# Score steps that divide blocks by four in place of six lower levels, in a chunked gated-linear-attention step on one core

## What is computed

```python
b = jnp.cumsum(gc, axis=2)
decay = jnp.exp(jnp.where(causal, b[:, :, :, None, :] - b[:, :, None, :, :], -jnp.inf))
scores = jnp.einsum('bhtd,bhsd,bhtsd->bhts', qc, kc, decay)
...
c = _split_cols(h @ w_in[l])
...
x = x + _rmsnorm(mix @ w_out[l], norm_post[l])
```

## Time and profile before

| | |
|---|---|
| median of 3 runs | 1036.46 us (1035.76 to 1039.31) |
| the profiled execution, its own time | 1035.77 us |
| its span in the profile | 1033.9 us |
| PE, DVE, ACT, POOL busy, share of the span | 96%, 58%, 42%, 36% |
| one middle tile (425.25 to 542.24 us) | 116.99 us |
| granted clock of PE over the span | 0.985 |

### The profile page before, as it was taken

One profiled execution on the slowest core, in us unless ns is written; L12 is line 12 of the kernel. 1 busy time (PEld: TensorE's weight loads), 2 busy tenths in 40 slices (PEclk: granted clock), 3 DMA queues, 4 the chain that ended last, 5 costly groups with the idle time before them and its releaser, 6 DMA issues.

```text
span 1033.9 us, 26901 instructions
## 1 busy us (share of the span) xinstructions
PE 992.6 (96%) x11652; PEld 737.4 (71%) x11652; DVE 594.5 (58%) x1047; ACT 434.0 (42%) x845; POOL 376.0 (36%) x510
## 2 busy tenths in 40 slices
PE   2997899999999999999999999999999999999997
PEld 2867577855886668865887668865887668866783
DVE  4997578635744466535745467445735467335564
ACT  6965454531533335431534325432534325333333
POOL 1224441174305550174305650174305641256200
PEclk9997699999999999999999999999999999999999
DMA  8820432001220013101220013101220013001011
GB/s 309 292 92 3 135 121 61 9 1 42 63 62 1 2 63 65 39 2 42 63 62 1 2 63 62 42 1 42 63 62 2 2 62 59 25 2 42 1 65 44
DMA packets 41527, 56.21 MB, mean 54 GB/s; under 512 B 27793, under 2 KB 28603, under 8 KB 41403
## 3 DMA queue, kind: packets, MB, share of 16 engines
q1 hardware_dynamic: 41411, 54.51, 17.1%
HBM read 38.44 MB, written 9.86 MB: 47 GB/s over the span
## 4 chain that ended last, share of the span: by engine, by line
PE 76%; DVE 14%; ACT 4%; DMA 3%; issue 2%; SPq 1%; POOL 0%; DVEq 0%; ACTq 0%
PE pj L688 37%; PE op L911 15%; PE pj L707 7%; PE sc L786 6%; DVE w_lo L1812 2%; DMA h_lo<-xres 2%; PE m L843 2%; PE m L891 1%; PE sc L931 1%; PE op L931 1%; PE sc L797 1%; DVE A L1928 1%; DVE X L2075 1%; PE pj L883 1%; DVE B L1865 1%
## 5 line engine op out<-in xcount | busy, mean ns | idle before, releaser
L688 PE MATMUL pj<-h_hi,w_hi 128*128 128x256 f16 (+1 forms) x1728 | 211.4, 266 | 0.7
L688 PE MATMUL pj<-h_lo,w_hi 128*128 128x256 f16 (+1 forms) x1728 | 210.4, 265 | 0.0
L688 PE MATMUL pj<-h_hi,w_lo 128*128 128x256 f16 (+1 forms) x1728 | 209.0, 264 | 0.0
L521 POOL TENSOR_TENSOR G<-B 128x256 f32<-128x256 f32 x112 | 78.9, 705 | 290.1 <-DVE B L1865 166.7
L1928 DVE COPY_PREDICATED A<-cu,sc 64x256 f32<-64x256 uint8 x192 | 102.6, 534 | 131.6 <-PE sc L786 129.2
L688 PEld LDWEIGHTS pj<-h_hi,w_hi 128*128 128x128 f16 x1728 | 151.7, 99 | 28.6 <-issue 4.4
L688 PEld LDWEIGHTS pj<-h_lo,w_hi 128*128 128x128 f16 x1728 | 158.7, 99 | 18.2
L688 PEld LDWEIGHTS pj<-h_hi,w_lo 128*128 128x128 f16 x1728 | 158.1, 99 | 17.8
L532 POOL TENSOR_TENSOR G<-G,Q 128x256 f32<-128x256 f32 x112 | 87.7, 783 | 113.9 <-issue 70.0
L1356 ACT ACTIVATE G<-G 128x512 f32<-128x512 f32 x112 | 69.1, 622 | 79.4 <-POOL G L522 79.3
L533 POOL TENSOR_TENSOR G<-G,K 128x256 f32<-128x256 f32 x112 | 92.4, 825 | 0.0
(11 more groups left out here) (289 smaller groups left out, 1357.9 us busy)
## 6 DMA issues: line engine op xcount, KB each, us to landing
xin<-in_x_prompt SPq DMA_DIRECT2D x17, 512.0 KB, 4.4
wo_hi<-in_w_units SPq DMA_DIRECT2D x16, 512.0 KB, 5.5
xres<-in_x_prompt SPq DMA_DIRECT2D x15, 512.0 KB, 3.6
out_y_prompt<-xres SPq DMA_DIRECT2D x14, 512.0 KB, 2.6
wo_lo<-in_w_units SPq DMA_DIRECT2D x12, 512.0 KB, 5.9
xres<-in_w_out SPq DMA_DIRECT2D x8, 256.0 KB, 3.0
gpost<-in_w_out SPq DMA_DIRECT2D x8, 256.0 KB, 4.7
m_hi<-in_state_gla SPq DMA_DIRECT2D x1, 512.0 KB, 8.7
```

The source lines that it names most:

```text
L521: pool.tensor_tensor(Gv[R], Bv[R], mid, ALU.subtract).then_inc(*give(pool, "gs", i, 2 * n + 1))
L688: m = pe.matmul(b[:, j * T:(j + 1) * T], w[:, k, col + 128 * j:col + 128 * j + 128], h[:, k, :], start=(n == 0 and k == 0), stop=(n == 2 a ...
```

## The change

From tile 2 on a branch has four score steps and the diagonal in place of seven levels and the diagonal. Step 0 is the old level of h = 64. Steps 1 to 3 divide blocks of 4w tokens into four parts of w tokens (`FOURS`: w = 16, 4, 1). With a the part of the key (0, 1 or 2), the middle token is the last of part a, and the queries are all later parts: three, two or one of them. So a step has 6 query pieces where two old levels had 4: the query operand is 768 elements wide for each partition, the key operand uses 384 of 512. In detail:

- POOL: for each of steps 1 to 3 four subtractions (384, 256, 128 and 384 elements) and four products of the same sizes. `exponents` and `factors` of a step now follow each other directly; no step's exponents are written ahead of the factors of the step before
- ACT: two exponentials for each step, 768 elements and 384
- PE: 16 matmuls of 96 columns for each step, in place of 2 x 16 of 32 columns
- DVE: six predicated copies for each step (3 x 2 of 384, 256 and 128 elements), with a wait of DVE for itself between the three pairs
- buffers: the three `G` become one region, and the other pair of `H` (free within the tile) is the second region; so `turn_x` now waits for the last of these steps
- the places of the steps between the projections change in the orders of PE, ACT, POOL and DVE

```diff
+FOURS = (None, 16, 4, 1)
+BY_FOUR = 2
...
+        def g_four(i, br, lv):
+
+            free = H[(i + 1) % 2][:, :].bitcast(F32)
+            t = (g_all[:, :], free)[(lv + br + 1) % 2]
+            return t[:, 0:512].rearrange("p (j t) -> p j t", j=2), t[:, 512:1280].rearrange("p (j t) -> p j t", j=2)
...
-                sp.wait_ge(*filled(i - 2, "c_z"))
+                sp.wait_ge(*at("sc", i - 1, 2 * at_score(i - 1, 1, 3) + 2))
...
+        def four_exponents(i, br, lv):
...
+            for a_ in range(3):
+                pool.tensor_tensor(later(queries, w, a_), from_[:, :, a_ + 1:4],
+                                   ends[:, :, a_:a_ + 1].broadcast_to([128, 128 // w, 3 - a_, w]), ALU.subtract
+                                   ).then_inc(*give(pool, "gs", i, n + a_ + 1))
+            if lv == 1 and br == 0:
+                pool.wait_ge(*at("sc", i, 2 * at_score(i, 0, 0) + 2))
+            pool.tensor_tensor(blocks(keys, w)[:, :, 0:3], ends[:, :, 0:3].broadcast_to([128, 128 // w, 3, w]),
+                               from_[:, :, 0:3], ALU.subtract).then_inc(*give(pool, "gs", i, n + 4))
+
+        def four_factors(i, br, lv):
+            (keys, queries), w, n = g_four(i, br, lv), FOURS[lv], factors_done(i, br, lv) - 4
+            pool.wait_ge(*at("ge", i, exps_done(i, br, lv) - 1))
+            for a_ in range(3):
+                v = later(queries, w, a_)
+                pool.tensor_tensor(v, v, blocks(q_of(i, br), w)[:, :, a_ + 1:4], ALU.mult
+                                   ).then_inc(*give(pool, "gm", i, n + a_ + 1))
+            pool.wait_ge(*at("ge", i, exps_done(i, br, lv)))
+            v = blocks(keys, w)[:, :, 0:3]
+            pool.tensor_tensor(v, v, blocks(k_of(i, br), w)[:, :, 0:3], ALU.mult).then_inc(*give(pool, "gm", i, n + 4))
...
+            if i >= BY_FOUR and 0 < lv < DIAG:
+                keys, queries = g_four(i, br, lv)
+                for c in range(2):
+                    for j in range(2):
+                        for hh in range(2):
+                            for u in range(2):
+                                n, col = 2 * c + u, (2 * c + j) * 128
+                                m = pe.matmul(half(SC[hh], u)[:, col:col + 96], half(keys, hh)[:, j, 64 * n:64 * n + 64],
+                                              half(queries, hh)[:, j, 96 * n:96 * n + 96], start=True, stop=True)
...
+            if i >= BY_FOUR and lv > 0:
+                keys, queries = g_four(i, br, lv)
+                for n, v in ((1, queries), (0, blocks(keys, FOURS[lv])[:, :, 0:3])):
+                    act.wait_ge(*at("gs", i, factors_done(i, br, lv) - n))
+                    act.activation(v, v, ACT.Exp, scale=SCALE[br]).then_inc(*give(act, "ge", i, exps_done(i, br, lv) - n))
+                return
...
+            elif i >= BY_FOUR and lv < DIAG:
+                w = FOURS[lv]
+                for a_ in range(3):
+                    cols = slice((0, 3, 5)[a_] * w, (3, 5, 6)[a_] * w)
+                    if a_:
+                        dve.wait_ge(*own(dve))
+                    for u in range(2):
+                        to = half(A, u)[:, :, 64 * u:64 * u + 64].rearrange("p k (g t) -> p k g t", t=4 * w)
+                        mk = half(masks4, u)[:, 96 * lv - 96:96 * lv].rearrange("p (g t) -> p g t", t=6 * w)
+                        from_ = half(sc, u).rearrange("p (k t) -> p k t", t=128)[:, :, 0:96]
+                        m = dve.copy_predicated(to[:, :, :, (a_ + 1) * w:4 * w],
+                                                mk[:, :, cols].unsqueeze(1).broadcast_to([64, 8, 16 // w, (3 - a_) * w]),
+                                                from_.rearrange("p k (g t) -> p k g t", t=6 * w)[:, :, :, cols])
```

More of the change, by code:

```diff
@@ L75, in fill_order @@
     for i in range(2, NT):
-        fills += [(i, n) for n in ("c_f", "a_q", "a_k", "vi0", "vi1", "c_q")]
-        fills += [(i, n) for n in ("d_v", "po", "d_z", "a_z", "b_c", "b_v", "b_b")]
-        fills += [(i + 1, "lr"), (i, "b_z"), (i + 1, "la"), (i, "c_z")]
+        fills += [
+            (i, "c_f"), (i, "a_q"), (i, "a_k"), (i, "vi0"), (i, "vi1"), (i, "c_q"), (i, "d_v"), (i, "po"),
+            (i, "d_z"), (i, "a_z"), (i, "b_c"), (i, "b_v"), (i, "b_b"), (i + 1, "lr"), (i, "b_z"), (i + 1, "la"),
+            (i, "c_z"),
+        ]
     fills += [
-        (NT, "c_f"), (NT, "a_q"), (NT, "a_k"), (NT, "vi0"), (NT, "c_q"), (NT, "vi1"), (NT, "d_v"),
-        (NT, "d_z"), (NT, "po"), (NT, "a_z"), (NT, "b_c"), (NT, "b_v"), (NT, "b_b"), (NT, "tails"),
-        (NT, "b_z"), (NT, "c_z"),
+        (NT, "c_f"), (NT, "a_q"), (NT, "a_k"), (NT, "vi0"), (NT, "c_q"), (NT, "vi1"), (NT, "d_v"), (NT, "d_z"),
+        (NT, "po"), (NT, "a_z"), (NT, "b_c"), (NT, "b_v"), (NT, "b_b"), (NT, "tails"), (NT, "b_z"), (NT, "c_z"),
     ]
@@ L173, in program @@
         gpost = sb("gpost", [128, D])
-        G = [sb(f"G{n}", [128, 2, TT]) for n in range(3)]
+        g_all = sb("G", [128, 6 * TT])
+        G = [g_all[:, 512 * n:512 * n + 512].rearrange("p (j t) -> p j t", j=2) for n in range(3)]
         A = sb("A", [128, 8, CH])
@@ L516, in exponents @@
                 pool.wait_ge(*at("qt", i, 0))
-            if n >= 3:
+            if i >= BY_FOUR and br:
+                pool.wait_ge(*filled(i - 1, "c_z"))
+            if n >= 3 and i < BY_FOUR:
                 per = len(levels(i))
@@ L618, in _ @@
             for i in range(2, NT):
[L619 to L631, removed]
+                exponents(i, 0, 0)
+                factors(i, 0, 0)
+                exponents(i, 0, 1)
+                factors(i, 0, 1)
+                exponents(i, 0, 2)
+                factors(i, 0, 2)
+                exponents(i, 0, 3)
+                factors(i, 0, 3)
+                key_exponents(i, 0)
+                exponents(i, 1, 0)
+                factors(i, 1, 0)
+                key_product(i, 0)
+                exponents(i, 1, 1)
+                factors(i, 1, 1)
+                exponents(i, 1, 2)
+                factors(i, 1, 2)
+                exponents(i, 1, 3)
+                factors(i, 1, 3)
+                key_exponents(i, 1)
                 key_product(i, 1)
@@ L2346, in _ @@
                 forget_sum(i)
[L2347 to L2348 removed]
+                copy_scores(i, 0, 0)
+                copy_scores(i, 0, 1)
+                copy_scores(i, 0, 2)
                 query_in(i)
[L2350 removed]
                 query_min(i)
                 query_silu(i)
[L2353 removed]
+                copy_scores(i, 0, 3)
                 copy_scores(i, 0, DIAG)
```

219 lines of the change are left out of this document (111 added, 108 removed).

## The result

| | before | changed |
|---|---|---|
| median | 1037.03 us (1035.76 to 1039.31, 4 runs) | 1094.67 us (1093.42 to 1097.66, 4 runs) |
| ratio | | 1.0557 [1.0527, 1.0588] |
| the profiled execution, its span | 1033.9 us | 1092.0 us |
| granted clock over the span | 0.985 | 0.961 |

The change makes the kernel 5.6% slower. The direction was forecast, the size was not: 1094.67 us lies above the range of 1047 to 1090. The span grew by 58.1 us, where the sum of the prediction had 33.9. Two more of its signs failed with it: PE's busy time was to be some 20 us lower and a middle tile near 122 us.

The account below looks back on a forecast made before the run. PE bounds the kernel, busy 116.06 of a middle tile's 116.99 us. The profiled 1035.77 plus 30.9 for six middle tiles and 3.0 for the last gave 1069.7, forecast as 1069 us; range 1047 to 1090.

Parts of the forecast that it names:

- the sum of the prediction: Middle tile: 7.95 us of waits less 2.8 saved, +5.1; six tiles +30.9 and the last +3.0.
- the small waits: Middle tile, PE: 0.1 us at step 2 of branch 1, and `updates` growing by about 0.6 from 0.47.
- What PE saves: Each tile loses 12 steps of 0.68 us and gains 6 of 0.90: 2.8 saved, between 2.0 and 3.8.
- Steps 1 and 2 of branch 0: Middle tile: step 1's exponential stands behind `values_out` on ACT, step 2's likewise; PE waits 1.95 us at each.
- Copies of step 3: On DVE, short runs of 3, 2 and 1 make the copies take 4.5 us with two waits for itself.
- rival of a small loss: Step 3's copies take 2.7 us, a step 0.74 on PE; +0.8 a tile, 1041 us; chance 0.10.
- the diagonal of branch 1: Middle tile: PE arrives 3.5 us after step 3 starts, DVE's copy ends at 5.5; wait 2.0 us.
- Diagonal of branch 0: Middle tile: step 3's copy ends 16.2 us after step 2 starts, PE needs 14.8; wait 1.35 us.
- Last tile: Waits of 2.0 us at the diagonal of branch 0 and 3.75 at step 2 of branch 1; +3.0 net.
- The clock falls: Rival: waits bring back 13 us at 1.2 GHz once a tile, costing 42 us in all, 1111; chance 0.05.
- the bounds of the step on PE: A step of 96 columns at 0.74 or 1.03 us, moving 84 steps by -13 or +11 us.

Follow-up runs that it names:

- e8: e6 with key_decays of branch 1 ahead of the gate of D on ACT and the next tile's input moved earlier on ACT and DVE: 1019.68 us, ratio 0.9813.
- e2: The changed kernel with the exponentials of steps 1 and 2 of branch 0 ahead of the value copies on ACT: 1063.67 us, ratio 1.0244.
- e4: The kernel before, with the exponentials of levels 1 and 2 of branch 0 put behind the first value copy on ACT: 1068.82 us, ratio 1.0274.
- e1: The changed kernel with surplus matmuls filling PE's three large waits in tiles 2 to 7: 1087.99 us, ratio 1.0482.
- e6: The changed kernel with nothing left out, instructions reordered on ACT, DVE and PE to suit the new steps: 1051.9 us, ratio 1.0132.
- e3: The changed kernel with step 3 copying only the first of its three pairs, some scores left out: 1071.04 us, ratio 1.031.

## Why the prediction missed

Two steps failed: the clock, which the sum put at nothing, and the small waits, which it made too short. Point by point, by its own steps:

- **What PE saves: right.** The step of 96 columns took 0.82 us (528.87 to 529.69), 0.90 with the entry of the earlier trace rows, as forecast. The estimate of 0.94 from the Trainium skill (TensorEngine Tiling (Array Packing), "Instruction Overhead") was a little high; the saving of 2.9 a tile in e8 goes with the row.
- **Steps 1 and 2 of branch 0: right.** 2.05 and 2.03 against 1.95 each, and the cause, ACT's order, is shown by e2 from one side and by e4 from the other.
- **Copies of step 3: right.** 4.47 us against 4.5, so the rival of a small loss falls. The wait of the diagonal of branch 1 was 2.39, not 2.0: DVE took up the copy 1.49 us after the start of the step (530.36 against 528.87), not 1.0, since a part of the gate of D stood ahead of it until then.
- **Diagonal of branch 0: right in its chain, wrong in the result.** The copy began 11.7 us after the start of step 2, as forecast, and ended at 496.56. PE should have waited 1.35 for it and waited nothing, since the slow matmuls made it late itself. In e1 and e2 the wait is there, 1.53.
- **Last tile: right in the waits, wrong in what follows.** The waits are 1.88 and 3.87 against 2.0 and 3.75, yet the tile grew by 5.8 us against 3.0. The matmuls behind the second wait took 4.30 us, not 2.63, and are 1.7 of it. Of the remaining 1.1, 0.67 is a wait for DVE (`tailB`, at 1054.92) that the kernel before hasn't; the rest has no cause found.
- **The clock: the step whose mechanism failed.** The rival "The clock falls" was priced as one stretch of 13 us a tile, 42 us in all, and given 0.05, because "the waits here stand apart, with matmuls between them". They do, and it doesn't help: the clock falls after a single wait of 2 us and comes back some 4 us later. The right price was some 1.65 us behind most of the waits, 23 us over six tiles, of which 13 covered other waits and 9.4 are net (e1). The Trainium skill (TensorE: Matmul & The Clock Gate, Part 1) has the sign of it, a clock that is halved after the engine was idle; its size, and that a wait of 2 us is enough, come from these rows.
- **The small waits: mis-sized.** With the clock full (e1) six tiles are 41.9 us longer than before (745.7 less 703.8), where 30.9 was forecast. The places are the diagonals (0.2 and 0.4 more a tile), step 2 of branch 1 (0.37 against 0.1), `updates` (1.36 against 1.07) and `attend`, which had not been looked at (0.55): 1.7 a tile, 1.9 with the 0.18 of steps 1 and 2. The tiles of e1 are 1.6 to 1.9 us longer than forecast, one 2.6 with a DMA wait of 0.9 in it.

So the 24.2 us that are missing from the sum are 11.0 of small waits, 9.4 net of the clock, 2.8 in the last tile and 1.1 ahead of tile 2. Either of the first two alone would have left the time below 1090; both together didn't. The range failed for the same reason: its upper end had 3 us for the clock, and no term by which all waits could be late together. It was even too wide by its own terms: the bounds of the step on PE were taken for 84 steps, where six in each of seven tiles are 42, so -7 and +5 us, not -13 and +11 (and the time by the Trainium skill's figure 2 us later, not 3).

What was not settled is which waits the clock falls behind. That of step 1 is 2.04 or 2.05 us long in every tile; from step 1 to step 2 PE then took 9.87 to 9.93 us in four tiles, and 8.23, as with the clock full, in tiles 2 and 6. No run tells these tiles apart.

## What to carry to other kernels

In this kernel a wait of PE of 2 us or more mostly cost more than its length: in another, look at the matmuls behind such a wait, and keep up to double its price in the range, less what other waits the delay would cover. When many small steps are merged into fewer and longer ones, redo the order of every engine around them: the exponentials (1.24 us for 0.62), products (3.1 for 1.4) and copies (2.75 for 0.88, 4.47 for 1.47) of a step are two to three times as long as those of a level and arrive late at places where the old ones just fitted, and here the same change went from +5.6% to -1.9% by moving instructions alone. And after each move ask what stood behind the moved instruction, as e6 did not.

## What the runs showed of the hardware

- After waits of PE of 2.0, 2.4, 2.8, 3.5 and 3.9 us the next 3 to 6 us of matmuls mostly ran slow, at a mean clock of 0.60 to 0.68 in the windows that hold little else; after the waits of up to 1.55 us in tiles 2 to 8 they did not (1.92 us for sixteen behind the 1.53, in e1).
- The same wait isn't always followed by it: beside the counts above (14 of 18 in the changed kernel, 2 of 6 in e2, 10 of 12 in e3, 6 of 6 in e4, 5 of 6 in e6), the window 994.00:1000.00 of the changed kernel, behind a wait of 1.88 us in the last tile, has a clock of 1.00, and the same place in e1 (985.00:990.00, wait 1.89) has 0.66. Executions of one kernel differ with the clock: by 10.3 to 10.6 us in e4.
- Predicated copies took longer with short runs of elements: six, 768 elements for each partition in all, took 4.47 us with runs of 3, 2 and 1 elements, and 2.74 to 2.77 with runs of 4 and more (steps 1 and 2).
- A step of 96 columns costs PE 0.82 us for its 32 records, where 64 columns cost 0.63 and 32 cost 0.60.
